# Later slots for the tails and value sums of a paged attention, and a branch norm done by parts

## The reference

```python
def decoder_layer(x, c, lw, conv_ctx, ssm_h0, ffn_ctx, k_past, v_past):
    mod = jax.nn.silu(c) @ lw['w_ada'] + lw['b_ada']
    sh1, sc1, g1, sh2, sc2, g2 = jnp.split(mod[:, None, :], 6, axis=-1)
    h = rmsnorm(x, lw['g_pre_mix']) * (1 + sc1) + sh1
    m, k_new, v_new, ssm_new, conv_new = mixer(h, lw, conv_ctx, ssm_h0, k_past, v_past)
    x = x + g1 * rmsnorm(m, lw['g_post_mix'])
    h = rmsnorm(x, lw['g_pre_ffn']) * (1 + sc2) + sh2
    f, ffn_new = conv_ffn(h, lw, ffn_ctx)
    x = x + g2 * rmsnorm(f, lw['g_post_ffn'])
    return x, (k_new, v_new, ssm_new, conv_new, ffn_new)

def sb_block(q, qpos, k, v, kpos, bias):          # the attention over pages
    z = einsum(q, k) * d ** -0.5 + bias
    log_1m = where(mask, log_sigmoid(-z), 0)
    tail = cumsum(log_1m, reverse=True) - log_1m  # sum over the later keys
    w = where(mask, exp(log_sigmoid(z) + tail), 0)
    return einsum(w, v)
```

## Time and profile before

| | |
|---|---|
| median of 3 runs (lowest, highest) | 1929.06 us (1926.95, 1942.0) |
| the profiled execution | 1934.29 us, its span 1932.1 us |
| mean granted clock of TensorE | 0.931 |
| busy: TensorE, VectorE, ScalarE | 1756.3, 1015.7, 661.2 us |
| HBM read, over the span | 377.03 MB, 201 GB/s |
| `whi` from `raw`, ScalarE L1355 | mean 1915 ns |
| `wlo`, VectorE L1683 | mean 2288 ns |

### The profile page before, as it was taken

How to read it: one execution, slowest core, us unless ns; L and a number is a source line. 1 busy time by engine, 2 the same in 40 slices (tenths; PEclk the granted TensorE clock), 3 DMA queues, 4 the chain that set the end, 5 groups by cost and what they waited for, 6 DMA issues and landing times.

```text
span 1932.1 us, 32035 instructions
## 1 busy us (share of the span) xinstructions
PE 1756.3 (91%) x13877; PEld 1572.5 (81%) x13877; DVE 1015.7 (53%) x1343; ACT 661.2 (34%) x648; POOL 57.3 (3%) x153
## 2 busy tenths in 40 slices
PE   5888989998677977988995999999999999999997
PEld 3766878886555655557884999999999999999996
DVE  2334444554656323454446566656556566565566
ACT  3333131213733332123224343333333333333344
POOL 3000000000000000010000100000000000000000
PEclk8989999999788885598997999999999999999999
DMA  9677796987368973046781444545454544545441
GB/s 340 241 252 268 261 327 240 329 310 276 118 228 308 350 277 127 1 142 218 262 280 68 153 165 163 170 158 175 155 173 156 171 161 166 166 162 172 156 153 66
DMA packets 183077, 389.50 MB, mean 202 GB/s; under 512 B 7635, under 2 KB 16067, under 8 KB 182641
## 3 DMA queue, kind: packets, MB, share of 16 engines
q1 hardware_dynamic: 179488, 375.68, 56.5%
q0 software_dynamic: 2752, 9.24, 1.4%
q10 hardware_dynamic: 698, 2.55, 0.4%
HBM read 377.03 MB, written 10.41 MB: 201 GB/s over the span
## 4 chain that ended last, share of the span: by engine, by line
PE 81%; DVE 8%; ACT 4%; DMA 3%; issue 2%; SPq 1%; DVEq 0%; ACTq 0%
PE ps L783 14%; PE ps L782 14%; PE ps L784 14%; PE ps L763 6%; PE ps L764 6%; PE ps L765 6%; PE ps L704 4%; PE ps L743 4%; PE ps L960 2%; PE ps L993 1%; SPq L450 1%; PE ps L1106 1%; DVE wlo L1683 1%; PE ps L1097 1%; DMA raw<-in_w_in_dram 1%
## 5 line engine op out<-in xcount | busy, mean ns | idle before, releaser
L1683 DVE TENSOR_TENSOR wlo<-raw,whi 128x2048 fp32r<-128x2048 f32 x146 | 332.9, 2288 | 198.0 <-ACT whi L1355 196.4
L782 PE MATMUL ps<-h2hi,whi 128*128 128x288 f32 x1408 | 417.3, 296 | 12.3 <-DVE wlo L1683 12.3
L1355 ACT ACTIVATE whi<-raw 128x2048 fp32r<-128x2048 f32 x145 | 277.5, 1915 | 436.2 <-PE ps L784 373.3
L783 PE MATMUL ps<-h2lo,whi 128*128 128x288 f32 x1408 | 417.9, 297 | 0.0
L784 PE MATMUL ps<-h2hi,wlo 128*128 128x288 f32 x1408 | 417.6, 297 | 0.0
L782 PEld LDWEIGHTS ps<-h2hi,whi 128*128 128x128 f32 x1408 | 268.4, 191 | 12.9 <-issue 11.9
L783 PEld LDWEIGHTS ps<-h2lo,whi 128*128 128x128 f32 x1408 | 265.4, 188 | 0.0
L784 PEld LDWEIGHTS ps<-h2hi,wlo 128*128 128x128 f32 x1408 | 265.2, 188 | 0.0
L763 PE MATMUL ps<-hhi,whi_in 128*128 128x288 f32 x704 | 209.6, 298 | 7.7 <-DVE wlo L1683 7.1
L764 PE MATMUL ps<-hlo,whi_in 128*128 128x288 f32 x704 | 209.1, 297 | 0.0
L765 PE MATMUL ps<-hhi,wlo 128*128 128x288 f32 x704 | 208.9, 297 | 0.0
(11 more groups left out here) (426 smaller groups left out, 2440.0 us busy)
## 6 DMA issues: line engine op xcount, KB each, us to landing
raw<-in_w_ffn_in_dram SPq DMA_DIRECT2D x88, 1024.0 KB, 5.0
raw<-in_w_ada_dram SPq DMA_DIRECT2D x84, 1024.0 KB, 8.5
raw<-in_w_in_dram SPq DMA_DIRECT2D x44, 1024.0 KB, 5.3
raw<-in_w_ffn_out_dram SPq DMA_DIRECT2D x44, 1024.0 KB, 5.0
kring<-in_cache_k_dram SPq DMA_DIRECT2D x64, 512.0 KB, 5.8
vring<-in_cache_v_dram SPq DMA_DIRECT2D x64, 512.0 KB, 5.4
raw<-in_w_out_dram SPq DMA_DIRECT2D x14, 1024.0 KB, 7.5
araw<-in_w_ada_dram SPq DMA_DIRECT2D x8, 1024.0 KB, 18.8
```

The source lines that it names most:

```text
L782: mm(o, high[:, q, cols], xh, start=(first and q == 0), stop=False)
L783: mm(o, high[:, q, cols], xl, start=False, stop=False)
L1355: fn(high_of(g), landed_at(u), ACT.Copy).then_inc(hi_ready, 1)
L1683: tt(low_of(u), landed_at(u), high_of(g).bitcast(F32), SUB).then_inc(lo_ready, 1)
```

## The change

In the attention everything from the tails on moves one slot later: `tails` and `log_weights` to n%8 = 4, `weights` and the row copies to 5, `summed` to 6, `LAG` from 12 to 13; there is one slot more at the end. In the output projection ScalarE squares a quarter of the branch and at once multiplies its prompt columns by the gain g1 x g_post_mix (`branch_part`), VectorE does so for the sample columns (`branch_samples`), and the gain itself is computed earlier. The first two FFN units are split in the last two products instead of behind the first two parts of `prepare`. Both norms' sums are made in column tiles, copied and added up (`norm_sums`, `sums_of_rows`). The branch is then scaled by r and added in one operation each. A few semaphores are merged: `c_T` and `fc_T` into `rows_T`, with the counts that follow; that moves no wait.

```diff
@@ constants and names @@
-        LAG = 12
+        LAG = 13
+        ssm_dma, g1_ready, m_gained = sem("ssm_dma"), sem("g1_ready"), sem("m_gained")
@@ TensorE @@
-            def norm_sums(sq, bank=5):
+            def norm_sums(sq):
                 norms[0] += 1
-                for k in range(KC):
-                    if k % 4 == 0:
-                        pe.wait_ge(sq_ready, 4 * (norms[0] - 1) + k // 4 + 1)
-                    i = mm(ps[:, bank, 0:T], ones[:], sq[:, k, :], start=(k == 0), stop=(k == KC - 1))
+                for p in range(4):
+                    pe.wait_ge(sq_ready, 4 * (norms[0] - 1) + p + 1)
+                    for j in range(4):
+                        i = mm(ps[32 * j:32 * j + 32, 5, 0:T], ones[:, 0:32], sq[:, 4 * p + j, :], start=(p == 0), stop=(p == 3))
                 i.then_inc(sum_ready, 1)
+                pe.wait_ge(rows_out, 7 + norms[0])
+                mm(ps[:, 4, 0:T], ones[:], rT[:], start=True, stop=True).then_inc(sum_ready, 1)
...
-                if n % NPG == 3 and 11 <= n < NPAGES + 11:
-                    tails((n - 11) // NPG)
+                if n % NPG == 4 and 12 <= n < NPAGES + 12:
+                    tails((n - 12) // NPG)
                 if LAG <= n < NPAGES + LAG:
                     page_sum(n - LAG)
-                if n % NPG == 4 and 20 <= n:
-                    sums_T((n - 20) // NPG)
+                if n % NPG == 5 and 21 <= n:
+                    sums_T((n - 21) // NPG)
@@ ScalarE @@
-                if n % NPG == 4 and LAG <= n < NPAGES + LAG:
+                if n % NPG == 5 and LAG <= n < NPAGES + LAG:
                     weights((n - LAG) // NPG)
-                if n % NPG == 4 and 20 <= n:
-                    rows_of_sums((n - 20) // NPG)
+                if n % NPG == 5 and 21 <= n:
+                    rows_of_sums((n - 21) // NPG)
...
+            def branch_part(p):
+                square(sq2, mT, parts=(p,))
+                act.wait_ge(g1_ready, 1)
+                act.wait_ge(sq_ready, 4 + p + 1)
+                for k in range(4 * p, 4 * p + 4):
+                    i = fn(mT[:, k, 0:SEQ], mT[:, k, 0:SEQ], ACT.Copy, scale=gainT[:, k, 0:1])
+                i.then_inc(m_gained, 1)
...
+                hi()
                 if n == QUARTERS * PROJ_GROUPS:
-                    hi()
                     roots()
-                elif n + 2 < QUARTERS * (PROJ_GROUPS + OUT_GROUPS):
-                    hi()
...
                 if q == 1 and g:
                     act.wait_ge(*evacuated(2 * n - 1))
-                    square(sq2, mT, parts=(g - 1,))
+                    branch_part(g - 1)
             act.wait_ge(pair_dve, ALL_DVE)
-            square(sq2, mT, parts=(3,))
-            root(5, rT[:], DM)
+            branch_part(3)
+            root(4, rT[:], 32 * DM, 2)
             square(sq2, xT, ready=lambda p: act.wait_ge(x2_ready, p + 1))
-            root(5, rT[:], DM)
+            root(4, rT[:], 32 * DM, 2)
             for p in range(4):
                 modulate(h2f[:, 4 * p:4 * p + 4], h2hi, SH2, p)
-                hi()
+                if p >= 2:
+                    hi()
@@ VectorE, prepare @@
                 c.mark(gain(scale, g, 1.0))
+                sums_of_rows(7)
...
                     if p:
                         low(p - 1)
-                        lo()
+                        if p == 3:
+                            lo()
@@ VectorE, attention @@
-                if n % NPG == 3 and 11 <= n < NPAGES + 11:
-                    log_weights((n - 11) // NPG)
-                if n % NPG == 5 and 21 <= n:
-                    summed((n - 21) // NPG)
+                if n % NPG == 4 and 12 <= n < NPAGES + 12:
+                    log_weights((n - 12) // NPG)
+                if n % NPG == 6 and 22 <= n:
+                    summed((n - 22) // NPG)
@@ VectorE, output projection and branch @@
+            def branch_samples(p):
+                part = slice(4 * p, 4 * p + 4)
+                dve.wait_ge(g1_ready, 1)
+                dve.wait_ge(sq_ready, 4 + p + 1)
+                c.mark(tt(smp(mT)[:, part], smp(mT)[:, part], per_seq(gainT)[:, part], MUL))
+
+            def sums_of_rows(n):
+                dve.wait_ge(sum_ready, n)
+                cp(rT[:], ps[:, 5, 0:T]).then_inc(rows_out, 1)
...
+                    if n == QUARTERS * PROJ_GROUPS + 2 * OUT_GROUPS:
+                        gain(G1, V_POST_MIX, 0.0).then_inc(g1_ready, 1)
...
-                    if n + 2 < QUARTERS * (PROJ_GROUPS + OUT_GROUPS):
-                        lo()
+                    lo()
+                    if q == 1 and g:
+                        branch_samples(g - 1)
...
-            def add_branch(m, gate, g):
-                c.mark(gain(gate, g, 0.0))
-                norms[0] += 1
-                dve.wait_ge(root_ready, norms[0])
-                c.link(dve.reciprocal(rT[:], rT[:]))
-                for p in range(4):
-                    part = slice(4 * p, 4 * p + 4)
-                    c.link(tt(m[:, part], m[:, part], rT[:].unsqueeze(1).to_broadcast([P, 4, T]), MUL))
-                    c.link(tt(smp(m)[:, part], smp(m)[:, part], per_seq(gainT)[:, part], MUL))
-                    for k in range(4 * p, 4 * p + 4):
-                        stt(xT[:, k, 0:SEQ], m[:, k, 0:SEQ], gainT[:, k, 0:1], xT[:, k, 0:SEQ], MUL, ADD)
-                    tt(smp(xT)[:, part], smp(xT)[:, part], smp(m)[:, part], ADD).then_inc(x2_ready, 1)
-            add_branch(mT, G1, V_POST_MIX)
+            branch_samples(3)
+            sums_of_rows(5)
+            norms[0] += 1
+            dve.wait_ge(root_ready, norms[0])
+            c.link(dve.reciprocal(rT[:], rT[:]))
+            dve.wait_ge(m_gained, 4)
+            for p in range(4):
+                part = slice(4 * p, 4 * p + 4)
+                c.link(tt(mT[:, part], mT[:, part], rT[:].unsqueeze(1).to_broadcast([P, 4, T]), MUL))
+                tt(xT[:, part], xT[:, part], mT[:, part], ADD).then_inc(x2_ready, 1)
```

More of the change, by code:

```diff
@@ L310, in hybrid_step @@
         ada_row, fold_full, mod_ready = sem("ada_row"), sem("fold_full"), sem("mod_ready")
-        c_T = sem("c_T")
         in_c, in_vec, in_ctx, in_x, in_misc = (sem(n) for n in ("in_c", "in_vec", "in_ctx", "in_x", "in_misc"))
@@ L353, in hybrid_step @@
         y_ready, y_dma = sem("y_ready"), sem("y_dma")
-        fc_T, fc_o = sem("fc_T"), sem("fc_o")
+        fc_o = sem("fc_o")
         (dt_na, dt_act, dA_full, dA_ready, ac_full, ac_out, ac_exp, xdt_made, dtE_full, eaE_made,
@@ L362, in hybrid_step @@
         ysrow_out, ys_T_full = sem("ysrow_out"), sem("ys_T_full")
-        ssm_dma = sem("ssm_dma")
+        ssm_dma, g1_ready, m_gained = sem("ssm_dma"), sem("g1_ready"), sem("m_gained")
         w_ada_v, w_in_v, w_out_v, w_fi_v, w_fo_v = w_ada[0], w_in[0], w_out[0], w_ffn_in[0], w_ffn_out[0]
@@ L793, in _ @@
                 i = tr(ps[:, 1, 256 + k * NSEQ:256 + (k + 1) * NSEQ], crow[:, k * P:(k + 1) * P], NSEQ)
-            i.then_inc(c_T, 1)
+            i.then_inc(rows_T, 1)
             pe.wait_ge(c_ready, 1)
@@ L1263, in conv_rows @@
                     i = tr(ps[:, 5 + n // 4, (n % 4) * P:(n % 4 + 1) * P], fcomp[:, n, :], P)
-                i.then_inc(fc_T, 1)
+                i.then_inc(rows_T, 1)
                 for r in range(2):
                     i = tr(ps[0:2 * FC, 4, r * P:(r + 1) * P], pcol[:, :, r], P)
-                i.then_inc(fc_T, 1)
+                i.then_inc(rows_T, 1)
             pe.wait_ge(f_lo, ROUNDS)
@@ L1306, in _ @@
             act.dma_start(vrow[V_CW:V_CB, 1, :], conv_w[0].rearrange("k (c p) -> (k c) p", p=P)).then_inc(in_vec, 16)
-            act.wait_ge(c_T, 1)
+            act.wait_ge(rows_T, 1)
             act.wait_ge(consts, 3)
@@ L1317, in square, with root @@
                     fn(dst[:, k:k + 4], src[:, k:k + 4], ACT.Square).then_inc(sq_ready, 1)
-            def root(bank, dst, width):
-                norms[0] += 1
-                act.wait_ge(sum_ready, norms[0] + 1)
+            def root(bank, dst, width, sums=1):
+                norms[0] += sums
+                act.wait_ge(sum_ready, norms[0])
                 fn(dst, ps[:, bank, 0:T], ACT.Sqrt, scale=1.0 / width, bias=eps[:]).then_inc(root_ready, 1)
@@ L1363, in _ @@
             act.wait_ge(consts, 3)
-            root(0, rT[:], 32 * DM)
+            root(0, rT[:], 32 * DM, 2)
             hi()
@@ L1631, in _ @@
                 if j == 1:
-                    act.wait_ge(fc_T, 2)
+                    act.wait_ge(rows_T, 5)
                     fn(fstage[:, 0:8].rearrange("p (b c) f -> p b (c f)", b=2), ps[:, 5:7, :], ACT.Copy)
@@ L1662, in vectors @@
             def vectors():
-                dve.wait_ge(rows_T, 1)
+                dve.wait_ge(rows_T, 2)
                 cp(vecT[:, 0, :], ps[:, 2, 0:P])
@@ L1667, in contexts @@
             def contexts():
-                dve.wait_ge(rows_T, 2)
+                dve.wait_ge(rows_T, 3)
                 rows = ctxT[:].rearrange("p (g c) r -> p c r g", c=11)
```

1 line of the change is left out of this document (removed).

## The result

The changed kernel takes 1919.0 us (median; 1913.6 to 1923.1), the kernel before beside it 1931.1. The ratio is 0.9927 with a 95% interval of 0.9909 to 0.9945: 14.1 us less (10.6 to 17.6), under 1% but clear of no change. The forecast from the median was 19.7 us less, to 1909. By the time alone the result lies nearer to rivals (a) and (b), at 1920 and 1920.7, than to the forecast; only the trace tells which of them happened. The profiled execution took a span of 1916.4.

What follows compares the result with a forecast made beforehand. TensorE carries 81% of the span, so its waits and half clock matter. Savings of 16.7 (attention) and 3.0 us (branch norm) sum to 19.7, from the median of 1929.06 to 1909; range 1895 to 1926.

Steps and rivals of the forecast that it cites:

- (a): Attention: the stall only moves to page transposes and scores, with the slow clock as now; 1920 us, chance 0.20.
- (b): Attention: page loads are already at their ceiling, so the 36 slots give 0; 1920.7 us, chance 0.08.
- part one: Paged attention: tails, weights and value sums a slot later save 16.7 us in sum.
- slots before 19: Attention's early slots: the first tail product did not wait, so the gain is 0, within 1 us.
- sequence 1: Attention's first long tail wait, 6.83 us: most of the stall moves, but later work comes earlier; 3.8 us gained (0 to 5).
- sequence 2: Attention's second long tail wait, 5.94 us: the stall moves likewise, what moves up saves 1.0 us.
- 36 slots: Attention's last 4.5 sequences, to the last scores: 23.8 us a sequence falls near the loads' 20.7; 11.3 us gained.
- drain: Attention's end: one more value sum lies in the shadow of the last suffix chain; 0.6 us gained.
- (c): Attention: slow clock goes too and TensorE sets the pace, 19 to 20 us a sequence; 1900 us, chance 0.18.
- Part two: Mixer branch's norm up to the first FFN product: 3.0 us gained, between 1.0 and 5.6.
- First root: Branch norm: shorter sums, but a later row copy and half clock, put the root 2.4 us later.
- FFN start: First FFN product: two weight units are ready, so it waits only for h's first low part; 2.7 us gained.

Runs made afterwards that it cites:

- e1: Only the attention's slots moved, branch norm as before, against the kernel before: 1919.7 us against 1934.4, ratio 0.9909.
- e3: The changed kernel with the first two FFN units' conversions back where they stood before: 1909.4 us, ratio 0.9872 to the kernel before.
- e2: Only the branch norm changed, attention slots as before, against the kernel before: 1933.3 us, ratio 1.0001.
- e9: The changed kernel with tails and `log_weights` back in their old slot, weights and value sums still later: 1939.3 us, ratio 1.0038 to the kernel before.
- e5: The changed kernel with VectorE's dt softplus and convolution pieces moved to other slots: 1919.9 us, ratio 0.9948 to the kernel before.
- e7: The changed kernel loading only heads 0 to 3 of V from page 4 on: 1911.3 us, ratio 0.9921 to the kernel before.
- e4: The changed kernel with the early FFN conversions put behind the row copy and branch squares: 1915.4 us, ratio 0.9894 to the kernel before.
- e11: The kernel before with transposes of two pages a sequence made twice from slot 34 on: 1927.9 us against 1930.3, ratio 0.9979.

## Why the prediction was right, and where its terms were off

The mechanism and the main term held. The terms of part one, from the starts of VectorE's page copies in the traces of before and after (the attention of after started 0.75 us later):

```
                                    forecast   measured
slots before 19                       0          2.5
sequence 1                            3.8        1.6
sequence 2                            1.0        0.9
36 slots, to the last scores         11.3       11.9
drain                                 0.6       -0.7
part one                             16.7       16.2
```

- *Slots before 19, "0, within 1"*: wrong. The step looked only for a wait at the first tails and found none. But moving the tails (at half clock there) out of slot 11 let VectorE have page 12 3.1 us sooner: its copies of pages 11 and 12 were 8.4 us apart and are 5.3, in the changed kernel, in e1 and in e3 alike, while in e2 and e9, with the tails in slot 11, they are 8.2 and 8.3 apart. 2.5 of it stayed.
- *Sequence 1, 3.8*: too much by 2.2, though the reason given fits: with VectorE's convolution pieces away (e5) the stand is gone and the sequence 25.0 us instead of 29.9. That the miss of one term covers that of the other is luck: the two terms together were forecast at 3.8 and gave 4.1.
- *Sequence 2*: as worked out. The stall moved to the transposes, as the list of signs said, at 4.9 and 4.0 us.
- *36 slots*: right in size: 23.2, 21.6, 20.8 and 20.6 us a sequence, at up to 406 GB/s. The forecast gave the slow clock 3.3 us and the waits 2.4, and left 2.5 of 5.6 on the loads. e2 and e9 bear out the clock's share (2.8 and 3.1 us of busy time). The waits that are left are for pages, as forecast, but their cause was not, or not only, the rate at which bytes come: with half of V away the sequence is only 0.2 to 1.3 us shorter (e7), and stands of 1.9 us stay, among them one of 1.11 for a K page. TensorE's own work is 18.4 to 18.7 us at full clock, not 18.2. So rival (c), under 20 us a sequence, failed for a reason other than the one held against it, 414 GB/s of supply; which it is stays open (e7).
- *Rival (b)*, 358 GB/s for a core by the Trainium skill, DMA: Bandwidth & Descriptors, section "Where 436 GB/s comes from": the traces of this one core disagree. 8.39 MB came in 20.59 us at 406 GB/s, and e2 held 408 over 21.03.
- *The drain*: off by 1.3. One wait of 2.0 us for the suffixes came back at the last tails.

So part one's sum, right within 0.5 us, is in part luck: its misses of 2.5, -2.2, 0.6 and -1.3 cancel. The one step of its reasoning that failed is that nothing before slot 19 would move.

Part two was forecast at 3.0 and is 1.4 in the trace to the first FFN product, 2.4 to the steady FFN. Its terms:

- *First root, -2.4*: measured -3.9 (14.29 to 18.19). The step had the row copy right (10 us after the last product: 9.6) and the sums at half clock (4.07 for "about 4"). It left the fold (1.0 taken, 1.87 measured) and the product with ones (0.8 taken, 1.33 measured) at full clock. Both stand in the same slow stretch.
- *Branch parts, 3.2*: 3.4. *Second sums, -0.5*: -0.9. *FFN start, 2.7*: 2.8, and no wait for `wlo`.

In the timings part two is nothing (e2), part one 17.6 (e1), both together 14.1 (10.6 to 17.6). These agree within their intervals. The traces give 16.2 and 1.4 to 2.4, at or just above the interval's upper end. The result is 5.6 us short of 19.7. Of that, 1.1 to 2.1 is in the terms above. In the two profiles the rest can be followed: the attention started 0.75 us later in after, so it ended 15.4 earlier (714.7 for 730.0), and the stretch from there to the Mamba output's squares, which no version touches, took 152.6 us for 150.1. That stretch took 149.7 to 153.5 from profile to profile, so what it gave back here is chance as far as one trace on each side tells.

The prediction did not price the early conversions by themselves: put early for 2.7 us at the FFN start, they cost 8.3 us at the root (e3). It had seen the row copy come later and the clock fall, but set them against the shorter sums and came to 2.4 for the two together, where 3.9 was measured. e4 shows that the price hangs on the place: behind the row copy it is 0.5.

## What to carry to other kernels

A wait of TensorE can cost more than its length where the granted clock falls behind it: before pricing it, compare TensorE's busy time for the same matmuls at both clocks (21.5 against 18.4 us in e9, at equal idle time). Moving a consumer a slot later pays where the producer's engines have nothing else late. Where they owe another copy to the same engine, the stall moves there, and moving the producer's other work took the stall along (e5). Work that is put early "beside" something stands ahead of all that its engine does next: place it behind the instruction for which the idle engine waits.

## What the runs showed that was not expected

- Two sequences with 16 more matmuls each were done 2.9 us sooner (e11), at a granted clock of 1.00 in place of 0.86. Two earlier ones, filled alike, were not.
- In both kernels, and with half of V taken away alike, SyncE issued the K and V loads 1.11 us apart when nothing held it, though one issue occupies it for 0.34. The queue of SyncE in the changed kernel:

```profile
646.01 0.34 SPq L484 DMA_DIRECT2D vring<-in_cache_v_dram  x1
647.12 0.34 SPq L478 DMA_DIRECT2D kring<-in_cache_k_dram  x1
648.23 0.34 SPq L484 DMA_DIRECT2D vring<-in_cache_v_dram  x1
649.35 0.34 SPq L478 DMA_DIRECT2D kring<-in_cache_k_dram  x1
```

  Sixteen of them take 17.8 us, not far below the 20.35 of a sequence. Whether this makes the 1.9 us of stands that are left was not tried (e7).
- One profile of an unchanged stretch isn't its time: the attention of before ended at 730.0, 729.1 and, in e2, 723.0.
